# Prenorm statistics of the next half inside the down-projection loop, with a w_ada ring of two buffers

## What is computed

```
mod = (jax.nn.silu(c) @ w_ada + b_ada).reshape(c.shape[0], N_MOD, 1, D_MODEL)
h = modulate(rms_norm(x, ln_ffn1_pre), sh1, sc1)
x = x + 0.5 * g1 * rms_norm(swiglu(h, ffn1_w_gate, ffn1_w_up, ffn1_w_down), ln_ffn1_post)
...
h = modulate(rms_norm(x, ln_ffn2_pre), sh2, sc2)
x = x + 0.5 * g2 * rms_norm(swiglu(h, ffn2_w_gate, ffn2_w_up, ffn2_w_down), ln_ffn2_post)
```

## Time and profile before

| | us |
|---|---|
| runs shown | 2368.78 and 2242.17, median 2305.47 |
| the profiled execution | 2248.01 |
| its span, slowest core (6) | 2245.6 |
| spans of the eight cores | 2213.1 to 2245.6 |

### The profile page before, as it was taken

The page is one execution under the profiler, slowest core; times in us unless marked ns, Lnnn a source line. Parts: engine busy times, 40 slices in busy tenths (PEclk is TensorE's granted clock), DMA queues, the critical chain, the costliest instruction groups (busy, mean ns, idle before and its releaser), DMA issues.

```text
span 2245.6 us, 24311 instructions; the slowest of 8 cores (2213.1 to 2245.6 us)
## 1 busy us (share of the span) xinstructions
PE 1430.6 (64%) x8150; PEld 669.5 (30%) x8289; DVE 744.5 (33%) x1270; ACT 661.5 (29%) x1066; POOL 324.9 (14%) x358
## 2 busy tenths in 40 slices
PE   0178889469995022554463454555439999479993
PEld 0034444134442001231131122123114444134441
DVE  0122210332103152662566377176342210432203
ACT  0221111411122003444454354344451111511121
POOL 0222221021100311121120112111001111001110
PEclk9989999689998555776775777677669999689997
DMA  7969996467852956862552356353234557446763
GB/s 178 109 62 122 130 89 66 54 63 84 92 52 27 156 51 111 78 61 24 56 50 26 34 52 61 33 56 38 26 45 57 76 64 68 85 77 75 83 65 88
DMA packets 454663, 158.46 MB, mean 71 GB/s; under 512 B 338704, under 2 KB 446224, under 8 KB 454544
## 3 DMA queue, kind: packets, MB, share of 16 engines
q0 software_dynamic: 423712, 130.31, 56.2%
q1 hardware_dynamic: 30832, 26.61, 4.3%
HBM read 274.13 MB, written 13.05 MB: 128 GB/s over the span
## 4 chain that ended last, share of the span: by engine, by line
PE 53%; DMA 13%; DVE 13%; issue 9%; ACT 9%; SPq 1%; POOL 1%; DVEq 0%; ACTq 0%; POOLq 0%
PE pb L181 52%; DMA wada<-w_ada 7%; DVE tmp L209 3%; DVE xT_sb L197 3%; DMA w_ring<-w_in 3%; DMA wo<-w_out 2%; DVE mtmp L209 2%; SPq L175 1%; DMA wd<-w_down 1%; ACT hy L192 1%; DVE TL L209 1%; ACT T L192 1%; ACT L192 1%; PE pb L185 1%; DVE Zs L213 1%
## 5 line engine op out<-in xcount | busy, mean ns | idle before, releaser
L181 PE MATMUL pb<-hy,wg 128*128 128x512 bf16 x1361 | 336.2, 388 | 14.3 <-ACT hy L192 11.4
L181 PE MATMUL pb<-hy,wu 128*128 128x512 bf16 x1382 | 333.9, 382 | 1.6 <-issue 0.2
L181 PE MATMUL pb<-actT,wd 128*128 128x512 bf16 x1378 | 312.8, 382 | 13.0 <-DMA wd<-w_down 11.5
L197 DVE TENSOR_TENSOR actT<-sg,pb 128x512 bf16<-128x512 f32 x176 | 121.0, 688 | 502.9 <-PE pb L181 486.0
L192 ACT ACTIVATE sg<-pb 128x512 f32<-128x512 f32 x176 | 105.1, 597 | 469.4 <-PE pb L181 452.2
L181 PE MATMUL pb<-mhT,w_ring 128*128 128x512 bf16 x752 | 186.8, 410 | 59.5 <-ACT mhT L192 56.8
L181 PEld LDWEIGHTS pb<-hy,wu 128*128 128x128 bf16 x1408 | 139.1, 99 | 170.8 <-issue 8.3
L181 PEld LDWEIGHTS pb<-actT,wd 128*128 128x128 bf16 x1408 | 137.4, 98 | 175.7 <-issue 15.5
L181 PEld LDWEIGHTS pb<-hy,wg 128*128 128x128 bf16 x1408 | 133.8, 99 | 165.9 <-issue 23.3
L175 POOL DMA_DIRECT2D w_ring<-w_in x120 | 105.6, 882 | 445.0 <-PE pb L181 383.8
L209 DVE SCALAR_TENSOR_TENSOR tmp<-hy,Gcoef,rstd 128x512 f32<-128x512 f32 x64 | 47.7, 746 | 356.3 <-ACT rstd L192 356.3
(11 more groups left out here) (198 smaller groups left out, 1502.6 us busy)
## 6 DMA issues: line engine op xcount, KB each, us to landing
w_ring<-w_in POOLq DMA_DIRECT2D x120, 256.0 KB, 6.3
wg<-w_gate POOLq DMA_DIRECT2D x44, 512.0 KB, 7.5
wu<-w_up POOLq DMA_DIRECT2D x44, 512.0 KB, 8.8
wd<-w_down POOLq DMA_DIRECT2D x32, 704.0 KB, 8.4
wada<-w_ada POOLq DMA_DIRECT2D x72, 256.0 KB, 7.7
wo<-w_out POOLq DMA_DIRECT2D x40, 256.0 KB, 4.6
xT_sb<-xT SPq DMA_DIRECT2D x4, 2048.0 KB, 30.2
yT<-xT_sb SPq DMA_DIRECT2D x4, 2048.0 KB, 6.9
```

Of the source, the lines that this page charges most:

```text
L181: self.op(self.pe, lambda e: e.matmul(_ap(out), _ap(lhsT), _ap(rhs), start=start, stop=stop), R=[lhsT, rhs], W=[out], inc=inc)
L197: self.op(eng, lambda e: e.tensor_tensor(_ap(out), _ap(in0), _ap(in1), op), R=[in0, in1], W=[out])
```

## The change

The squares and sums of blocks 2 and 3 become a generator, `prenorm_stats_gen`, of which one step is taken after each of the 16 down groups of half 0, into banks 0 and 1; the rest is run out after the post norm of block 0. The scale and shift part is `prenorm_mod`. The four `sq` buffers are split, two for the down loop, two for all prenorm squares. `rstd` gets a third buffer, and the w_ada ring has two in place of three.

```diff
-            rstd = [SB(f"rstd{fi}_{i}", [128, 512], F32, fs) for i in range(2)]
+            rstd = [SB(f"rstd{fi}_{i}", [128, 512], F32, fs) for i in range(3)]
...
-                mod_state["ring"] = [SB(f"wada{i}", [128, 8, 128], BF16, fs) for i in range(3)]
+                mod_state["ring"] = [SB(f"wada{i}", [128, 8, 128], BF16, fs) for i in range(2)]
...
+            def prenorm_stats_gen(blk, r, bank):
                 cols = slice(blk * 512, (blk + 1) * 512)
+                prev = None
                 for c in range(8):
-                    s = sq[cnt["q"] % 4]
-                    cnt["q"] += 1
+                    s = sq[2 + cnt["qp"] % 2]
+                    cnt["qp"] += 1
                     kb.A(s[:], Sl(xT[:, c, cols], blk), AF.Square)
-                    kb.mm(pb[4][:, :], ones_d[:], s[:], start=(c == 0), stop=(c == 7), inc=True)
-                r = rstd[cnt["r"] % 2]
-                cnt["r"] += 1
-                kb.rsqrt(r[:], pb[4][:, :], eps_col[:])
+                    if prev is not None:
+                        kb.mm(bank[:, :], ones_d[:], prev[1][:], start=(prev[0] == 0), stop=False, inc=True)
+                    prev = (c, s)
+                    yield
+                kb.mm(bank[:, :], ones_d[:], prev[1][:], start=False, stop=True, inc=True)
+                yield
+                kb.rsqrt(r[:], bank[:, :], eps_col[:])
+                yield
...
+            def prenorm(blk, bi):
+                for _ in prenorm_stats_gen(blk, rstd[bi], pb[4]):
+                    pass
+                prenorm_mod(blk, bi, rstd[bi])
...
+                def nxt_stats():
+                    if half == 0:
+                        yield from prenorm_stats_gen(2, rstd[0], pb[0])
+                        yield from prenorm_stats_gen(3, rstd[1], pb[1])
+                gen = nxt_stats()
...
-                        s = sq[cnt["q"] % 4]
+                        s = sq[cnt["q"] % 2]
                         cnt["q"] += 1
                         kb.A(s[:], py[:], AF.Square)
+                        next(gen, None)
...
-                    r = rstd[cnt["r"] % 2]
-                    cnt["r"] += 1
+                    r = rstd[2]
                     kb.rsqrt(r[:], stp, eps_col[:])
...
                     if half == 0 and bi == 0:
-                        prenorm(2, 0)
-                        prenorm(3, 1)
+                        for _ in gen:
+                            pass
+                        prenorm_mod(2, 0, rstd[0])
+                        prenorm_mod(3, 1, rstd[1])
```

More of the change, by code:

```diff
@@ L387, in ffn, with prenorm_mod @@
             wd_v = wd_d[fi].rearrange("(j p) n -> p j n", p=128)
-            cnt = {"n": 0, "m": 0, "q": 0, "t": 0, "r": 0}
-            def prenorm(blk, bi):
+            cnt = {"n": 0, "m": 0, "q": 0, "t": 0, "r": 0, "qp": 0}
+            def prenorm_stats_gen(blk, r, bank):
                 cols = slice(blk * 512, (blk + 1) * 512)
+                prev = None
                 for c in range(8):
-                    s = sq[cnt["q"] % 4]
-                    cnt["q"] += 1
+                    s = sq[2 + cnt["qp"] % 2]
+                    cnt["qp"] += 1
                     kb.A(s[:], Sl(xT[:, c, cols], blk), AF.Square)
-                    kb.mm(pb[4][:, :], ones_d[:], s[:], start=(c == 0), stop=(c == 7), inc=True)
-                r = rstd[cnt["r"] % 2]
-                cnt["r"] += 1
-                kb.rsqrt(r[:], pb[4][:, :], eps_col[:])
+                    if prev is not None:
[6 more added lines that the diff above has]
+                yield
+            def prenorm_mod(blk, bi, r):
+                cols = slice(blk * 512, (blk + 1) * 512)
                 for c in range(8):
```

## The result

The changed kernel takes 2301.6 us, the kernel before 2244.1, as medians of all 11 and 10 executions; the ratio is 1.0247, 95% interval 1.0208 to 1.0285. It is slower, as forecast (2310, range 2284 to 2334, against 2248.0 for the execution the sum was made on).

A forecast was written before the change was run, and what follows sets the result against it. In FFN 1's gate loop TensorE and the DMA engines were taken as full, with w_ada landing last. Ring 43.8, clock 15.3, start 10, squares 4.8, turns -10.4 gave 63.5 on 2248.0: 2311.5, stated as 2310, range 2284 to 2334 us.

The forecast's parts named there:

- The ring in the gate loops with the clock: Gate loops of FFN 1: piece b1 waits 5.8 us at eleven pairs, +43.8 us; slower clock after these waits, +15.3.
- Rival A: Gate loops of FFN 1: w_ada lands sooner, so two buffers cost 0; 2242 or 2233 us; chance 6%.
- B: Gate-loop waits come but the clock does not fall, and the start is bound by rate: +43, 2291 us; chance 18%.
- C: Gate loops of FFN 1: half of the 22 other pieces also miss, by 1 to 2 us; 2334 us; chance 13%.
- First sixteen pieces: w_ada pieces ahead of the first prenorm: 3.53 us per piece with two in flight, 49.4 us for 14, +10.
- Square buffers: Four prenorms of half 0: square c + 1 waits for the matmul of square c - 1; 1.2 us each, +4.8.
- The turns: Between the halves of FFN 1 and FFN 2: the 7.36 us wait for block 3's rstd goes, -8.0 us per turn.
- Down loops: 13 `ones_d` matmuls move from TensorE's idle time into the TensorE-bound down loop: +2.8 us, net -5.2 per turn.

The follow-up runs named there:

- the filler: The changed kernel with 16 matmuls whose result nobody reads put ahead of the second piece of each step: 1.0222 against the kernel before.

## Why the prediction was right

The direction, the mechanism and the size held: 63.5 us by the sum, 58.1 between the median spans, 55.5 by the ratio. That it came so near owes something to luck, as terms were off in both directions. Step by step:

- *The ring in the gate loops with the clock:* 43.8 + 15.3 = 59.1 forecast; the loops grew by 46.1 in half 0 and 6.7 in half 1, 52.8. The waits in half 0 grew by 43.5 - 11.5 = 32.0, not 9 x 4.06 = 36.5, as the late piece ran at T + 11.1 in the median and not at T + 12.4. Why its DMA landed sooner was not tried; the DMA share, 0.88 where I read 1.06, goes with it. The clock took its part: 5.9 against 4.06 is 1.9 for each of nine waits, where I had 1.7; it holds for waits of 2 to 4 us too, which I had not counted on. Nine times 1.9, less some 2 that the kernel before already lost in half 0, is 15, and 32 + 15 = 47 is the measured 46. The ring alone and the filler show both.
- *Rival A* (two buffers are enough) is refuted by the ring-only run; *B* (no clock loss) by the filler; *C* (a second wait per step) by the count of 11 or 12 waits.
- *First sixteen pieces:* +10 forecast, +12.1 measured, but both ends were off. From the first issue to the last piece I had 49.4 against 39.3; the medians are 46.7 and 34.6, as core 6, whose rows I read, was among the slowest two there. On it 13 pieces in 39.3 are 3.02 each, too, and not the 2.85 of my model, so "as seen" was wrong. The landing with two in flight, which I took at 6.0, is 5.1 in the median on core 3. The last of the sixteen, forecast near 103, ran at 93 to 98.
- *Square buffers:* 1.2 for each prenorm forecast, 1.4 measured, and the run with that edit alone gives it.
- *The turns:* -8.0 each forecast; -8.4 and -7.8. *Down loops:* +2.8 each forecast; +1.8 and +1.6. On the quickest cores FFN 2's loop went from 83.0 to 85.6, 0.2 for each of 13 matmuls, as forecast; the medians grew less, as more cores had waited for wd before (four of eight, by 1.0 to 3.8 us; two in the changed kernel). Only the absorbed part was mis-sized.
- *Missed:* one rstd buffer for both post norms makes block 1's rsqrt wait for block 0's post norm where nothing lay between them. The shortest tail of the eight cores is 35.5 in all four runs with one buffer and 34.6 in all with two. Missed as well: the start, below.

## What to carry to other kernels

A buffer taken from a prefetch ring to make room is an edit of its own: read off how long that transfer takes in the loop as it is (queued behind the large ones, not alone), compare it with the time the remaining buffers leave, and count what the wait does to TensorE's clock as well. Before moving a load in the queue, ask which request will then stand behind the large ones, and whether fewer bytes would do more than a better order (here -5 us by order, -11 more by bytes in one loop). Work that is taken off a serial stretch is worth the full idle time only if what queues behind it is needed there: moving 14 us of VectorE work behind the gate's release took 17 us off the stretches, the statistics 5.

## What the runs showed that I had not expected

The first w_ada piece runs 1 to 4 us sooner with two buffers than with three: 48.6 to 49.7 us in the four runs with two, 50.5 to 52.7 in the seven with three (medians over cores). What is fetched ahead of it shares the DMA engines with cT, for which ScalarE waits there; that cause was argued, not tried.

The waits that cost clock are shorter than I thought. On the eight cores of the kernel before, none of the waits for w_ada below 1.9 us was followed by a slow group, some of 1.93 to 2.8 us were and some (2.25, 2.53) were not. In half 0 of the changed kernel 53 of 54 were (cores 0 to 5), and in the run with only the ring of two all 72 (mean 4.4 us). The 1.9 us is no lower bound: in the filler's run waits of 1.49, 1.51 and 1.68 us were followed by a group of 5.79 in place of 4.10, others of 1.5 to 1.7 were not.

A slower TensorE cost this loop next to nothing. On cores 6 and 7 of the changed kernel's profiled execution the granted clock stood between the usual 0.5 and 1 for most of the gate loop of half 0 (0.81 from 160 to 200 us on core 6), and pieces without a wait stood 4.4 and 4.8 us apart in place of 3.65 and 4.06. Yet the loop took 242 and 249 us there, against 239 to 257 on the other six, as the waits for w_ada shrank to 24 and 27 us from 43.5: the late DMA sets the pace there. It is one execution, and nothing was run to test it.
